# Expert stage of a hybrid decoder step: the down weights go through ScalarE's DMA queue, the gate and up weights stay on SyncE's

## The reference

```python
h = layer_norm(ALPHA * x + mix, ln1_g, ln1_b)
...
for gi in range(N_EXPERT_GROUPS):
    a = jnp.einsum('bld,edf->blef', h, w_gate[gi])
    b = jnp.einsum('bld,edf->blef', h, w_up[gi])
    act = jax.nn.silu(a) * b * gate[:, :, gi, :, None]
    y = y + jnp.einsum('blef,efd->bld', act, w_down[gi])
```

## Time and profile before

| | |
|---|---|
| median of three runs | 1270.48 us |
| the profiled execution, device time | 1273.31 us |
| its span | 1271.5 us, mean granted clock of TensorE 0.929 |
| expert passes | from about 877 to 1171 us of the span |
| busy | PE 86%, PEld 53%, DVE 35%, ACT 16%, POOL 18% |
| DMA | 190.44 MB, of which 163.87 MB in SP's queue (q1), 19.09 MB in GpSimd's (q0), 6.74 MB in ACT's (q10) |
| HBM | 162.68 MB read, 28.42 MB written |

### The profile page before, as it was taken

The page is one execution under the profiler, slowest core; times in us unless marked ns, Lnnn a source line. Parts: engine busy times, 40 slices in busy tenths (PEclk is TensorE's granted clock), DMA queues, the critical chain, the costliest instruction groups (busy, mean ns, idle before and its releaser), DMA issues. The chain is left out here.

```text
span 1271.5 us, 15878 instructions
## 1 busy us (share of the span) xinstructions
PE 1098.8 (86%) x6462; PEld 675.6 (53%) x6462; DVE 450.8 (35%) x764; ACT 199.9 (16%) x389; POOL 230.3 (18%) x244
## 2 busy tenths in 40 slices
PE   7999999999858999999999999403999999998473
PEld 5866666555547787777878765201333333332231
DVE  0233333230035656666656634540111111111056
ACT  0122222111022022112112100000111111111011
POOL 0000000110031032032122310051111111101037
PEclk9699999999969999999999998655999999999787
DMA  6011111112160111111111410484799999997184
GB/s 242 1 33 33 36 46 34 34 33 97 50 222 26 34 51 50 33 51 48 42 49 42 117 35 8 160 340 149 278 388 415 422 417 384 398 400 279 62 301 154
DMA packets 61780, 190.44 MB, mean 150 GB/s; under 512 B 10008, under 2 KB 37176, under 8 KB 52184
## 3 DMA queue, kind: packets, MB, share of 16 engines
q1 hardware_dynamic: 48384, 163.87, 34.0%
q0 software_dynamic: 8208, 19.09, 4.0%
q10 hardware_dynamic: 5136, 6.74, 1.5%
HBM read 162.68 MB, written 28.42 MB: 150 GB/s over the span
## 5 line engine op out<-in xcount | busy, mean ns | idle before, releaser
L324 PE MATMUL pj<-xT,wblk 128*128 128x384 f32 (+1 forms) x960 | 299.9, 475 | 12.3 <-DMA xT<-in_xt_dram 8.8
L324 PEld LDWEIGHTS pj<-xT,wblk 128*128 128x128 f32 x960 | 184.7, 193 | 124.6 <-issue 17.7
L1501 PE MATMUL e<-wgu_s,xgT 128*32 128x512 f32 x384 | 171.2, 599 | 0.0
L1501 PE MATMUL e<-wgu_a,xgT 128*32 128x512 f32 x768 | 115.0, 602 | 6.4 <-DVE xgT L1609 4.0
L1501 PE MATMUL e<-wdn_a,acT 128*32 128x512 f32 x576 | 86.8, 592 | 0.7 <-ACT acT L1570 0.7
L1501 PE MATMUL e<-szT,acT 128*32 128x512 f32 x192 | 86.3, 592 | 0.0
L1487 PE MATMUL e<-cst,xg 128*128 128x128 f32 x200 | 28.7, 291 | 64.7 <-DMA xg<-h_dram,lst 48.3
L1501 PEld LDWEIGHTS e<-wgu_a,xgT 128*32 128x32 f32 x768 | 31.9, 111 | 76.6 <-issue 71.9
L1614 DVE SCALAR_TENSOR_TENSOR ac<-sg,lst,e 128x256 f32<-128x256 f32 x24 | 11.5, 481 | 172.0 <-ACT sg L1566 172.0
L748 PE MATMUL b<-wout,ybt 128*128 128x512 f32 x144 | 68.6, 621 | 0.3 <-DVE logits L1107 0.3
L748 PE MATMUL b<-wout,yaT 128*128 128x512 f32 x144 | 65.7, 593 | 0.0
(11 more groups left out here) (300 smaller groups left out, 1497.8 us busy)
## 6 DMA issues: line engine op xcount, KB each, us to landing
wgu_a<-in_w_gate_up_dram SPq DMA_DIRECT2D x17, 2048.0 KB, 22.3
wdn_a<-in_w_down_dram SPq DMA_DIRECT2D x25, 1024.0 KB, 13.9
wgu_s<-in_w_gate_up_dram SPq DMA_DIRECT2D x8, 2048.0 KB, 15.5
qkvT<-in_w_gate_up_dram SPq DMA_DIRECT2D x8, 2048.0 KB, 19.5
wblk<-in_wcol_dram SPq DMA_DIRECT2D x20, 512.0 KB, 3.5
szT<-in_w_down_dram SPq DMA_DIRECT2D x8, 1024.0 KB, 18.0
picked<-picked_dram SPq DMA_DIRECT2D x8, 1024.0 KB, 6.4
stage<-qkvT SPq DMA_DIRECT2D x9, 512.0 KB, 3.6
```

What stands on the lines that cost most here:

```text
L324: last = pe.matmul(pj[par][:, bank * 512:bank * 512 + m], wblk[par][:, k, :], xT[:, k, a:a + m], start=(k == 0), stop=(k == KT - 1))
L1501: last = pe.matmul(out[at, :], lhsT[:, at], theirs if j == GROUP - 1 else mine, start=start, stop=stop)
```

## The change

The loads of the down weights in the expert stage, own and shared, are issued from ScalarE's queue, in its turn for pass q, between the copy of the output of pass q - 1 and the copy of acT. Since that output copy waits for down of pass q - 1, no further wait is needed for the slot (pass q + 2 takes the slot of pass q - 1). SyncE keeps the gate and up loads and no longer waits for `dn_done`. The loads of the routing stage, those of shared expert 1 and those of the overflow pass stay on SyncE.

```diff
-        def load_own_dn(q):
-            sp.dma_start(wdn_a[q % NA], dn_rows(own(q))).then_inc(dn_a_in[q % NA], 16)
+        def load_own_dn(q, queue=sp):
+            queue.dma_start(wdn_a[q % NA], dn_rows(own(q))).then_inc(dn_a_in[q % NA], 16)
...
-        def load_shared_dn(g):
-            sp.dma_start(wdn_s[g % ND], dn_rows(shared(g))).then_inc(dn_s_in[g % ND], 16)
+        def load_shared_dn(g, queue=sp):
+            queue.dma_start(wdn_s[g % ND], dn_rows(shared(g))).then_inc(dn_s_in[g % ND], 16)
...
                     for q in range(NA, NPASS):
                         e.wait_ge(gu_done, q - NA + 1)
                         load_own_gu(q)
-                        e.wait_ge(dn_done, q - NA + 1)
-                        load_own_dn(q)
                         g = (q + 1) // (GROUP - 1)
                         if q % (GROUP - 1) == GROUP - 2 and g < NE // GROUP:
                             load_shared_gu(g)
-                            load_shared_dn(g)
                     for t in range(NT):
                         sp.dma_start(hres[:, t, :], h_d[t * P:(t + 1) * P, :]).then_inc(hres_in, 16)
...
                             wait(e, scattered[(q - 1) % 2], 16 * ((q - 1) // 2))
                             out_s(e, q - 1, (q - 1) % 2)
+                        later = q + NA - 1
+                        if q >= 1 and later < NPASS:
+                            load_own_dn(later, act)
+                            g = (later + 1) // (GROUP - 1)
+                            if later % (GROUP - 1) == GROUP - 2 and g < NE // GROUP:
+                                load_shared_dn(g, act)
                         ac_turned_s(e, q, q % 2)
```

## The result

| | before | after |
|---|---|---|
| median of 20 runs each, on one chip | 1270.66 us | 1275.14 us |
| lowest to highest | 1266.62 to 1274.95 | 1269.82 to 1277.63 |
| ratio after/before, 95% interval | | 1.0026 [1.0013, 1.0038] |
| profiled execution: device time, span | 1273.31, 1271.5 us | 1269.82, 1267.9 us |

What follows compares the result with a forecast made beforehand. The prediction took DMA engines to limit the expert stage from 930 to 1140 us, by 1 to 2 us a group. Its terms, -4.9 + 9.8 - 1.3 = +3.6 us, added to the 1270.48 median gave 1274.1 us; range 1268.0 to 1279.5.

Steps and rivals of the forecast that it cites:

- The sign and its mechanism: Expert stage: slower, +3.6 us in sum, because a third queue makes TensorE wait for gathers; slower got 0.56.
- The price of a turn: DMA engines serve queues packet by packet in turn, whatever the size: estimated 0.615 us for 16 KB, 0.16 for 4 KB.
- Term 5: Expert-stage DMA queues: gate/up and down weights each take a turn, delaying gathers; +9.8 us, less 1.3 for rows left later.
- two loads ahead: Gate/up weights at stage end: two loads fetched before needed while gather rows waited, costing 2 x 4.9 = +9.8 us.
- 28 us from issue to use: A group's first gate/up load goes out about 28 us before use and lands 8 to 17 us early.
- Term 1: SyncE drops its wait for down; the shared gate/up load moves into unused DMA time of 890 to 950: -4.9 us.
- The later ones meet engines that are already full: Expert stage: gate/up loads after the earlier shared one gain nothing, so only one load's 4.9 us counts.
- Terms 2 to 4: 27 issues on ScalarE, its scatter wait also holding down loads, and nine earlier hres loads: 0 us each.
- grow from 6.4 to about 10: TensorE's holes in the expert stage become gather waits and grow from 6.4 to about 10 us.
- the clock rival: Fewer, longer gather waits drop TensorE's clock twice, 5 us on top: 1279 us; chance 0.10.
- Gathers keep up: Expert stage: down queue empties soon, gathers land in time, earlier gate/up loads remove all four holes: 1264.1 us; chance 0.12.
- No change: Expert-stage waits change name but keep their sum: 1268.0 to 1273.0 us; chance 0.32.

Runs made afterwards that it cites:

- e2: The changed kernel with SyncE's old wait for down put back between gate/up loads: third queue without the early order; 1279.97 us, ratio 1.0069 to before.
- e8: The changed kernel again, unedited, run for a second profile; 1275.26 us.
- e3: The changed kernel with each gate/up load cut into four DMAs with rows of 4 KB instead of 16; 1271.78 us, ratio 1.0005 to before.
- e1: The kernel before, all loads still on SyncE's queue but issued in the order their slots come free; 1264.05 us, ratio 0.9945 to before.
- e5: The kernel before with only the shared gate/up load moved ahead of the wait for down; 1269.54 us, ratio 0.9984 to before.
- e6: The kernel before with only the own gate/up loads moved ahead of the wait for down, on SyncE's queue; 1264.21 us, ratio 0.9942 to before.
- e4: The changed kernel with GpSimd issuing each gather ahead of the scatter that it followed; 1268.55 us, ratio 0.998 to before.
- e7: The kernel before with GpSimd issuing each gather ahead of the scatter that it followed; 1271.74 us, ratio 0.9998 to before.

## Why the prediction was right

The forecast was 1274.1 us, slower, and the runs gave 1275.14. The sign and its mechanism held; one term was put on the wrong load, and the form of the loss was only half foreseen. That the figure came so near is in part luck: the early order gained 1.9 us more than forecast and the third queue on top of it cost 1.8 to 2.6 us more, and these two errors cancel.

- **The price of a turn** is shown: equal turns for three queues (328, 335 and 334 packets, e2), gathers at 19.4 us where 18 or more was to be seen (17.8 in the second profile, e8), and 9.6 when the big packets are cut to 4 KB (e3).
- **Term 5, the third queue, +8.5 us.** Measured alone it is +9.1 (e2), and on top of the early order 10.3 to 11.1 (after against e1). The sum was near; its working, two loads ahead, was not measured by itself. What the runs do show is that gate/up loads land after 12.7 us and none is waited for any more, while the gathers are. With the prediction's 28 us from issue to use, a load then lies ready for some 15 us, more than a pass (an estimate).
- **Term 1, the early order, -4.9 us.** Mis-sized and misplaced: it is -6.8 (e1). The shared load did move, from 927.20 to 908.10 in after (911.8 when the stage's earlier start of 3.7 us is put back; the forecast said about 912). But moving it alone fills 2.4 us of DMA time and gives only 1.6 us (e5). The step that failed is "The later ones meet engines that are already full": the own loads, 4 to 6 us earlier, alone fill 5.4 us (e6) and gain 6.9, and the group's first own load was the one that was late.
- **Terms 2 to 4, 0 us each.** ScalarE's timeline of after shows the issues under their cover:

```profile
1031.97 0.60 ACT L1572 ACTIVATE yo<-e 128x512 f32<-128x512 f32 x1 [3.11 <-PE e L1498]
1031.98 0.33 ACTq L1185 DMA_DIRECT2D wdn_a<-in_w_down_dram  x1
1032.35 0.46 ACTq L1191 DMA_DIRECT2D szT<-in_w_down_dram  x1
1032.86 0.39 ACT L1567 ACTIVATE acT<-e 128x256 f32<-128x256 f32 x1 [0.28 <-issue]
```

The 27 issues take 0.33 to 0.59 us each, not 2.25, and acT still ends TensorE's wait only in the last pass, for 0.68 us, which before has too. ScalarE's hold on the scatter costs nothing as long as scatters come first; e4 shows what it costs when they do not. The hres loads leave no other hole at the end.
- **The holes "grow from 6.4 to about 10".** Not as written: they are 5.9 and 6.6 us in the two profiles. But the clock's half level adds 3.4 / 2 = 1.7 us in the first and 10.2 / 2 = 5.1 in the second, together 7.6 and 11.7. So the holes as such cost no more than before; what is lost against before is in large part the clock's. The forecast and the clock rival came together, as one case. A simple sum goes the same way. Without holes the stage takes 1157.24 - 874.23 = 283.0 us (e6). With holes and half the low-clock time added, before is 289.4 (measured 290.4), after 290.6 (292.2), e8 294.7 (295.0), e2 283.0 + 12.0 + 5.1 = 300.1 (1178.26 - 875.83 = 302.4). The measured stages are 0.3 to 2.3 us longer than the sums. Up to 0.9 us of that lies in the first passes: behind the 48 us without work ahead of them the granted clock is 0.50 in every kernel here, for 7.0 us of the stage in e6 and 8.7 in e2. The rest, 1.1 us in after and 1.4 in e2, stays open.
- **The rivals.** "Gathers keep up", 1264.1 us, is what happens with the early order and no third queue (e1, 1264.05): its time was right, its condition wasn't met. "No change" fails: the time rose by 0.26%, and e2 makes the third queue's part 0.69%. The Trainium skill (DMA: Bandwidth & Descriptors, section "Issuing engines are not separate DMA queues") says that the DMAs of all issuing engines run on the same 16 DMA engines, and that initiating on several only saves the time to initiate. On the first the trace agrees: the three queues share them, 54.4 + 28.5 + 15.2 = 98.1% in after. On the second it differs: e2 moves loads to another issuing engine and loses 9.1 us.

## What to carry to other kernels

Here one more DMA queue with work was one more packet in everyone's turn (e2). Where the DMA engines are full, ask which small transfers share them, and how long a row of the others' is, before loads are spread. A load that waits in a queue behind another load's wait is better freed by ordering that one queue by the time at which the slots come free (e6: 0.9942 of before) than by a second queue. And where two effects of a change nearly cancel, a run with each alone shows both.

## What was not expected of the hardware

A short hole of TensorE can cost more than itself, and not every hole does. Two holes of nearly the same length, in before (2.39 us, ended at 1060.63) and in e5 (2.25 us, ended at 1128.65), both at gate/up; the stretch of 3.4 us that begins some 0.3 us ahead of the end of each, of before and then of e5:

```profile
1060.30:1063.70 3.40, 3.07 (x32) 1.19 (x36) 0.00 (x0) 0.00 (x0) 0.65 (x1) 1.00 1.03 412
```

```profile
1128.30:1131.70 3.40, 3.05 (x16) 0.90 (x20) 0.00 (x0) 0.00 (x0) 0.00 (x0) 0.50 1.04 392
```

The longer was followed by the full clock, the shorter by half of it. Of the eight other holes of over 2 us in after, e2 and e8, six (2.06; 2.01, 2.66 and 2.75; 2.49 and 3.12 us) were followed by 3.4 or 6.8 us at the lower level, and two (2.18 in after, 2.25 in e2) were not. In e3 a hole of 2.75 us and in e7 one of 2.07 were followed by it, and one of 2.51 in e7 was not; in the 7.43 us of e3 the clock fell within the hole. After what holes this happens, and why not after all, these runs leave open. The other surprise is how little the shared load gained by itself, an early transfer of 2 MB while the engines had time to spare: it was not the one that anyone waited for.
